# A parallel-head decoder step on 8 cores: the order of the opening phase rewritten (x tiles, first weights, units in pieces)

## The reference

```python
h = rmsnorm(x, norm_g)                      # 4096 channels
z = h @ w_in                                # 9728 columns: u, gate_a, glu_val, glu_gate, gate_b, q, gate_c
a = glu_val * sigmoid(glu_gate)             # then a causal depthwise conv of width 31, layer norm, silu, @ w_pw
k, v = rmsnorm(mem, mem_norm_g) @ w_mem_k, ... @ w_mem_v      # 256 memory tokens
y = rmsnorm(x + concat(pool(u)*silu(gate_a), conv(a)*silu(gate_b), attn(q,k,v)*silu(gate_c)) @ w_out)
```

## Time and profile before

| | us |
|---|---|
| median of 3 runs | 1980.24 (1979.48 to 1980.29) |
| the profiled execution, its time | 1981.93 |
| its slowest core (core 4), first to last instruction | 1980.4 |
| the other cores | 1962.9 to 1976.2 |
| TensorE busy on core 4 | 1853.8 |
| VectorE busy | 971.4 |
| ScalarE busy | 357.1 |
| DMA, mean rate | 131 GB/s |

### The profile page before, as it was taken

How to read it: one execution, slowest core, us unless ns; L and a number is a source line. 1 busy time by engine, 2 the same in 40 slices (tenths; PEclk the granted TensorE clock), 3 DMA queues, 4 the chain that set the end, 5 groups by cost and what they waited for, 6 DMA issues and landing times.

```text
span 1980.4 us, 29544 instructions; the slowest of 8 cores (1962.9 to 1980.4 us)
## 1 busy us (share of the span) xinstructions
PE 1853.8 (94%) x11388; PEld 941.7 (48%) x11592; DVE 971.4 (49%) x1367; ACT 357.1 (18%) x626; POOL 142.0 (7%) x270
## 2 busy tenths in 40 slices
PE   2768999899999999999999999999989999999997
PEld 1435555555444544544445555554444444444443
DVE  4548898848888888898580111121000110000355
ACT  4531011011011111011141232321000111111222
POOL 0000010110000000000001111100010000000000
PEclk9989999999999999999999999999999999999999
DMA  8854977695535444445446999745469577556897
GB/s 231 245 130 77 169 131 128 112 170 100 92 67 90 91 80 76 87 80 100 69 61 94 154 147 151 117 70 99 86 106 188 172 154 157 115 130 146 220 302 240
DMA packets 82091, 259.20 MB, mean 131 GB/s; under 512 B 12224, under 2 KB 18496, under 8 KB 76352
## 3 DMA queue, kind: packets, MB, share of 16 engines
q0 software_dynamic: 39328, 153.76, 48.6%
q1 hardware_dynamic: 42624, 103.53, 16.9%
HBM read 370.56 MB, written 40.45 MB: 208 GB/s over the span
## 4 chain that ended last, share of the span: by engine, by line
PE 88%; DMA 5%; DVE 3%; issue 2%; ACT 1%; DVEq 0%; SPq 0%; ACTq 0%; POOLq 0%
PE pz L364 77%; PE ps L364 10%; DMA slot<-w_in 2%; DVE HT L444 2%; DMA wo<-w_out 1%; ACT XN L425 1%; DMA XT<-x 1%; DMA slot<-w_mem_v 1%; PE ps L442 0%; DVE SQ L376 0%; DVE YB L497 0%; PE pz L442 0%; DVE CCA L386 0%; DVE HM L444 0%; ACT XN L420 0%
## 5 line engine op out<-in xcount | busy, mean ns | idle before, releaser
L364 PE MATMUL pz<-HT,slot 128*128 128x512 bf16 x4715 | 1132.6, 382 | 17.6 <-DMA slot<-w_in 3.9
L386 DVE SCALAR_TENSOR_TENSOR YB<-EA,CS,YB 128x512 f32<-128x512 f32 x720 | 480.5, 745 | 0.0
L364 PEld LDWEIGHTS pz<-HT,slot 128*128 128x128 bf16 x4864 | 331.3, 98 | 311.1 <-issue 21.2
L364 PE MATMUL ps<-HT,slot 128*128 128x64 bf16 (+1 forms) x2432 | 469.4, 199 | 5.1 <-ACT SGt L370 3.6
L364 PEld LDWEIGHTS ps<-HT,slot 128*128 128x128 bf16 x2432 | 233.6, 98 | 287.2 <-issue 13.5
L376 DVE TENSOR_TENSOR YT<-pz,XR 128x512 f32<-128x512 f32 (+1 forms) x54 | 37.3, 691 | 283.9 <-PE pz L364 236.6
L340 POOL DMA_DIRECT2D slot<-w_in x152 | 80.8, 533 | 1004.4 <-PE ps L364 757.6
L364 PE MATMUL pz<-wo,CCA 128*128 128x512 bf16 (+1 forms) x636 | 148.9, 382 | 1.7 <-ACT SGC L370 0.8
L364 PE MATMUL pz<-wo,CCB 128*128 128x512 bf16 (+1 forms) x635 | 147.7, 379 | 0.7
L370 ACT ACT_TABLE_LOAD x45 | 57.7, 1283 | 477.0 <-PE ps L364 245.1
L1000 ACT ACTIVATE JK<-YT 128x512 bf16<-128x512 f32 (+1 forms) x72 | 45.3, 630 | 436.7 <-DVE YT L376 436.7
(11 more groups left out here) (148 smaller groups left out, 1190.9 us busy)
## 6 DMA issues: line engine op xcount, KB each, us to landing
slot<-w_in POOLq DMA_DIRECT2D x152, 512.0 KB, 6.2
wo<-w_out POOLq DMA_DIRECT2D x32, 1024.0 KB, 18.4
XT<-x SPq DMA_DIRECT2D x8, 2048.0 KB, 13.8
XR<-x SPq DMA_DIRECT2D x64, 256.0 KB, 8.1
y<-YT SPq DMA_DIRECT2D x64, 256.0 KB, 8.2
YF<-y SPq DMA_DIRECT2D x24, 512.0 KB, 6.6
y<-YF SPq DMA_DIRECT2D x24, 512.0 KB, 9.3
slot<-w_mem_k POOLq DMA_DIRECT2D x16, 512.0 KB, 9.1
```

Source lines behind the costliest of these rows:

```text
L364: S.op("pe", lambda e: e.matmul(out, lhsT=lhsT, rhs=rhs, start=start, stop=stop), r=r, w=w, t=max(64, n) / 2400 + 0.0025)
L386: S.op("dve", lambda e: e.scalar_tensor_tensor(out=out, in0=a, scalar=s, in1=b, op0=op0, op1=op1), r=r, w=w, wa=wa, t=n / 960 + 0.13)
```

## The change

- x has three buffers XT (the third in the place of HM) and XN has three. Tile 8, the one of 96 tokens, comes first: in the new order n = 0 is tile 8, n = 1 to 8 are tiles 0 to 7, n = 9 and 10 are memory. norm_scale(n) issues the load of n + 3. The first load is issued ahead of the constants, the second when those have landed, the third when the first tile has.
- Two more slots lie where the pooling's buffers will be; they are used once. w_gate lets POOL issue slot loads two at a time: each time after the load of tile n = 2, 4, 6, 8 has landed.
- The first three units are gg0, vv0 and gg1 (u0 goes back to the planner's list). They run in pieces of 256 tokens, for tiles 6 and 7 of 128, and one of 96, each between transposes. The small parts of the evictions (halo and samples: gg_small, v_small) are written right behind the piece of 96, the main ones at the end.
- vv1 is run as the fourth unit, ahead of the planner's loop, which starts with pair 2. norm_scale and norm_transpose of the memory tokens are written behind it.
- ESA's first load is issued behind the first tile, the pooling weights' load behind the opening.

```diff
-        XT = [at("XT", R, [D], F32), at("XT", R + 16384, [D], F32)]
+        XT = [at("XT", R, [D], F32), at("XT", R + 16384, [D], F32), at("XT", R_YB + 5 * 4352, [D], F32)]
         XN, XNb = [], []
-        for i, oo in enumerate((R_YB + 4352, R_YB + 3 * 4352)):
+        for i, oo in enumerate((R_YB + 4352, R_YB + 3 * 4352, R_AT + 5440)):
             XN.append(raw("XN", oo, [D], BF16)[0])
             XNb.append([S.buf("XN%d_%d" % (i, h), [(oo + 4096 * h, oo + 4096 * h + 4096)]) for h in range(2)])
         IDF, IDFb = at("IDF", R_AT, [128], F32)
+        slots += [at("slot", R_AT + 13632 + 4096 * i, [2048], BF16) for i in range(2)]
 
...
-        free_slots = collections.deque(range(NSLOT))
+        wst = {"issue": 0, "get": 0, "limit": 0}
+        free_slots = collections.deque((0, 1, 2, 3, NSLOT, NSLOT + 1, 4, 5))
         load_slot = {}
 
         def w_fill():
             if recording:
                 return
-            while free_slots and wst["issue"] < len(loads):
+            while free_slots and wst["issue"] < min(len(loads), wst["limit"]):
                 k = wst["issue"]
                 wst["issue"] += 1
                 name, i = loads[k]
@@ -351,7 +352,8 @@
         def w_release(s):
             if recording:
                 return
-            free_slots.append(s)
+            if s < NSLOT:
+                free_slots.append(s)
             w_fill()
 
...
-        S.dma("sp", lambda e: e.dma_start(out=CS[:], in_=cs_d), w=[CSb])
-        S.dma("sp", lambda e: e.dma_start(out=IDF[:], in_=id_d), w=[IDFb])
-        S.op("dve", lambda e: e.tensor_copy(out=IDB[:], in_=IDF[:]), r=[IDFb], w=[IDb])
         S.op("dve", lambda e: e.memset(ONES[:], 1.0), w=[ONb])
-
-        def norm_load(i, src, rows):
-            b = i % 2
-            S.dma("sp", lambda e: e.dma_start(out=XT[b][0][0:rows, :], in_=src), w=[XT[b][1]])
-
-        def norm_scale(i, rows):
-            b = i % 2
-            xt, xtb, xn, xnb, nb = XT[b][0], XT[b][1], XN[b], XNb[b], NSTb[i]
+        ORD = (8, 0, 1, 2, 3, 4, 5, 6, 7, 9, 10)
+        TILES = [(x_d[128 * i:min(NT, 128 * i + 128), :], min(NT - 128 * i, 128)) for i in range(9)]
+        TILES += [(mem_d[0:128, :], 128), (mem_d[128:256, :], 128)]
+
+        def norm_load(n):
+            if n < 11:
+                src, rows = TILES[ORD[n]]
+                S.dma("sp", lambda e: e.dma_start(out=XT[n % 3][0][0:rows, :], in_=src), w=[XT[n % 3][1]])
+
...
+            xt, xtb, xn, xnb, nb = XT[n % 3][0], XT[n % 3][1], XN[(n + n // 9) % 3], XNb[(n + n // 9) % 3], NSTb[i]
...
+            norm_load(n + 3)
+
+        def norm_transpose(n, qs):
+            i, rows = ORD[n], TILES[ORD[n]][1]
+            xn, xnb = XN[(n + n // 9) % 3], XNb[(n + n // 9) % 3]
+            if i < 9:
+                gcol, dst, dstb, c0 = C_G, HT, HTb[i], 128 * i
+            else:
+                gcol, dst, dstb, c0 = C_MG, HM, HMb[i - 9], (i - 9) * 128
+            for q in qs:
+                if i < 9:
                     k = ps()
                     t16, tb = PS16[k], PSb[k]
                 else:
...
+        def gg_small(j, si):
+            b = j % 2
+            act(EA[b][:, 0:NH], PS[si][:, 0:NH], AF.Sigmoid, [PSb[si]], [EAb[b][0]], NH)
+            act(SGS[b][0][:], PS[si][:, NH:NH + NS], AF.Sigmoid, [PSb[si]], [SGS[b][1]], NS)
+
...
+        def v_small(j, si):
             b = j % 2
             ea = EAb[b][0]
             tt(EA[b][:, 0:NH], PS[si][:, 0:NH], EA[b][:, 0:NH], ALU.mult, [PSb[si], ea], [], NH, wa=[ea])
             tt(ESA[:, :, 30:34], PS[si][:, NH:NH + NS].rearrange("p (s r) -> p s r", s=16),
                SGS[b][0][:].rearrange("p (s r) -> p s r", s=16), ALU.mult, [PSb[si], SGS[b][1]], [ESAb], NS)
+
+        def v_main(j, zi):
+            b = j % 2
+            ea = EAb[b][0]
             tt(EA[b][:, NH:], PZ[zi][:, :], EA[b][:, NH:], ALU.mult, [PZb[zi], ea], [], NPR, wa=[ea])
...
+        def w_gate(n, upto):
+            S.deps("pool", [XT[n % 3][1]], [])
+            wst["limit"] = upto
+            w_fill()
+
+        norm_load(0)
+        S.dma("sp", lambda e: e.dma_start(out=CS[:], in_=cs_d), w=[CSb])
+        S.dma("sp", lambda e: e.dma_start(out=IDF[:], in_=id_d), w=[IDFb])
+        S.op("dve", lambda e: e.tensor_copy(out=IDB[:], in_=IDF[:]), r=[IDFb], w=[IDb])
+        S.deps("sp", [CSb], [])
+        norm_load(1)
+        S.deps("sp", [XT[0][1]], [])
+        norm_load(2)
+        FIRST = (U_GG, U_V, U_GG + 1)
+        fs = {}
+        rot["pz"] = 3
+
+        def piece(u, a, b):
+            if u not in fs:
+                fs[u] = [w_get("in", 2 * FIRST[u] + h) for h in range(2)]
+            if b == NT:
+                k = ps()
+                out, tb = PS[k][:, 0:NT - a], PSb[k]
             else:
-                norm_transpose(i, 128, C_MG, HM, HMb[i - 9], (i - 9) * 128, False)
-
-        stage_load()
-        stage_load()
+                k = None
+                out, tb = PZ[u][:, a:b], PZb[u]
+            for kc in range(32):
+                sl = fs[u][kc // 16]
+                view = slots[sl][0][:, :].rearrange("p (k n) -> p k n", k=16)
+                mm(out, view[:, kc % 16, :], HT[:, kc, a:b], kc == 0, kc == 31, [slots[sl][1]] + HTb[a // 128:(b + 127) // 128], [tb])
+            return k
+
+        def whole(n):
+            norm_scale(n)
+            norm_transpose(n, range(4))
+
+        whole(0)
+        esa_load(0)
+        whole(1)
+        w_gate(2, 2)
+        whole(2)
+        norm_scale(3)
+        norm_transpose(3, (0, 1))
+        w_gate(4, 4)
+        piece(0, 0, 256)
+        norm_transpose(3, (2, 3))
+        gg_small(0, piece(0, NPR, NT))
+        norm_scale(4)
+        norm_transpose(4, range(4))
+        piece(0, 256, 512)
+        w_gate(6, 6)
+        piece(1, 0, 256)
+        piece(1, 256, 512)
+        v_small(0, piece(1, NPR, NT))
+        whole(5)
+        whole(6)
+        piece(0, 512, 768)
+        piece(1, 512, 768)
+        w_gate(8, 8)
+        gg_small(1, piece(2, NPR, NT))
+        piece(2, 0, 256)
+        norm_scale(7)
+        norm_transpose(7, (0, 1))
+        piece(2, 256, 512)
+        norm_transpose(7, (2, 3))
+        piece(2, 512, 768)
+        norm_scale(8)
+        norm_transpose(8, (0, 1))
+        piece(0, 768, 896)
+        norm_transpose(8, (2, 3))
+        piece(1, 768, 896)
+        piece(2, 768, 896)
+        wst["limit"] = 1 << 30
+        for u in range(3):
+            piece(u, 896, 1024)
+            for sl in fs[u]:
+                w_release(sl)
+            if u == 0:
+                gg_main(0, 0)
+            elif u == 1:
+                v_main(0, 1)
+            else:
+                gg_main(1, 2)
         wp_load(0)
-        esa_load(0)
...
         eus_load(0)
-        first_seg(1, 1, NPR, 1, 1)
-        first_seg(2, 1, NPR, 2, 0)
-        first_seg(0, 2, NPR, 0, 0)
-        for s_ in fs[0:2]:
-            w_release(s_)
-        gg_evac(0, 0, 0)
-        first_seg(1, 2, NPR, 1, 1)
-        for s_ in fs[2:4]:
-            w_release(s_)
-        sync_est("dve")
-        v_evac(0, 1, 1)
-        first_seg(2, 2, NPR, 2, 0)
-        for s_ in fs[4:6]:
-            w_release(s_)
-        u_evac(0, 2, 0)
-        rot["ps"] = 1
-        tile_T(9)
-        tile_T(10)
-        S.t["dve"] = S.t["pe"]
+        S.t["dve"] = S.t["pe"] + 7.0
...
+        run_unit("vv", 1)
+        for n in (9, 10):
+            norm_scale(n)
+            norm_transpose(n, range(4))
+        al = collections.deque(a_units)
         kl = collections.deque(kv_units)
         ql = collections.deque(range(8))
-        j = 1
+        j = 2
```

More of the change, by code:

```diff
@@ L441, in norm_transpose @@
                     kc = q * 8 + k
-                    S.op("pe", lambda e, k=k, kc=kc, tv=tv: e.transpose(out=tv[:, k, 0:rows], in_=XN[b][0:rows, kc * 128:(kc + 1) * 128],
-                                                                        identity=IDB[0:rows, 0:rows]), r=[XNb[b][q // 2], IDb], w=[tb], t=0.06)
+                    S.op("pe", lambda e, k=k, kc=kc, tv=tv: e.transpose(out=tv[:, k, 0:rows], in_=xn[0:rows, kc * 128:(kc + 1) * 128],
+                                                                        identity=IDB[0:rows, 0:rows]), r=[xnb[q // 2], IDb], w=[tb], t=0.06)
                 S.op("dve", lambda e, q=q, tv=tv: e.tensor_tensor(
@@ L473, in esa_load, with gg_main @@
             S.dma("sp", lambda e: e.dma_start(out=ESA[:].rearrange("p s r -> p (s r)"), in_=scin_d[j]), w=[ESAb])
+        def gg_small(j, si):
+            b = j % 2
+            act(EA[b][:, 0:NH], PS[si][:, 0:NH], AF.Sigmoid, [PSb[si]], [EAb[b][0]], NH)
+            act(SGS[b][0][:], PS[si][:, NH:NH + NS], AF.Sigmoid, [PSb[si]], [SGS[b][1]], NS)
+        def gg_main(j, zi):
+            b = j % 2
+            act(EA[b][:, NH:NH + NPR], PZ[zi][:, :], AF.Sigmoid, [PZb[zi]], [], NPR, wa=[EAb[b][0]])
         def gg_evac(j, zi, si):
-            b = j % 2
             if j >= 2:
                 bg_need("conv%d" % (j - 2))
[L479 to L483, removed]
```

(29 more changed lines are left out.)

11 lines of the change are left out of this document (1 added, 10 removed).

## The result

| | before | after |
|---|---|---|
| median, us | 1980.26 | 2027.21 |
| ratio, with its 95% interval | | 1.0236 [1.0213, 1.0259] |
| the profiled execution, us | 1981.93 | 2028.07 |
| its slowest core (core 4), us | 1980.4 | 2026.5 |
| the eight cores, us | 1962.9 to 1980.4 | 2007.7 to 2026.5 |

The change costs 47 us. The forecast was 1998 (1983 to 2007): the sign was right, the size was not, and the time lies outside the range. Beside the ratio to the kernel before I give the mean of the eight cores' spans, averaged over executions: for most kernels it scatters by only 1 us, while the slowest core scatters by several.

The account below looks back on a forecast made before the run. TensorE, busy 1853.8 of 1980.4 us, was taken as the bound, with most winnable idle time in the opening. The opening's +17.4 and +0.4 behind it gave 1980.2 + 17.8 = 1998.0 us, range 1983 to 2007.

Parts of the forecast that it names:

- The term: Opening: four units and all tiles done at 191.1, where before four would be at 173.7; +17.4 us.
- the two causes: Opening: squares of later tiles queue behind small gate evictions on ScalarE; memory norm's reciprocal queues behind v_evac(1) on VectorE.
- First transpose at 9.8 + 7.9: Opening: first tile and constants there at 9.8, its first transpose 7.9 later, at 17.7.
- the next follow at 8.75: Opening: the next tiles are transposed at a cadence of 8.75, at 25.5, 34.3 and 43.0.
- The first two slots are issued at n = 2's landing, about 24, and have 20 us: Opening: the first unit's two weight-slot loads go out at about 24 and have 20 us.
- the tables: ScalarE, opening: each activation table switch costs the load's 1.28; four new switches on the chain are in the sum.
- switches cost double: Rival: a table switch between waiting instructions costs the load's length again, 5.1 more; time 2003, chance 0.05.
- The cold start: TensorE, opening: a piece begun at the lower clock takes 2.2 more; four such starts, 8.8 in the sum.
- Behind the opening ... I take +0.4 for all this: After the opening: new unit order, w_mem_v slot waits that stay and four gate-unit neighbours; +0.4, bounds −2 and +3.
- Memory norm hidden: Rival: the memory tokens' reciprocals get ahead of v_evac(1), 7.9 less; time 1990, chance 0.08.
- Cadence holds: Rival, opening: relief of the transfers decides and TensorE stays warm, 17.8 − 21.1 = −3.3; time 1976, chance 0.12.
- Absorbed: Rival: the opening's loss is given back where TensorE waits later, behind 160 us; time 1980, chance 0.07.

Follow-up runs that it names:

- e2: Changed kernel with norm_scale of n = 4, 5 and 7 written ahead of the pieces whose evictions they stood behind: ratio 1.0148, mean of cores −15.4.
- e3: Changed kernel with norm_scale(9) ahead of the fourth unit and norm_scale(10) between its matmuls and its eviction: ratio 1.0198, mean −5.8.
- e10: Changed kernel with the rest of conv1 written behind v0, ahead of v1: ratio 1.014, mean −19.0.
- e11: Changed kernel with w_out's first tiles laid over the weight slots in the order in which they come free: ratio 1.0202, mean −8.0.
- e6: Kernel before with its own opening, then the units in the changed kernel's order: ratio 1.007, mean of cores +13.3 against before.
- e7: Changed kernel with its own opening, then a list giving the units in the order of the kernel before: ratio 1.0158, mean −18.4.
- e8: Changed kernel with the edits of e2, e3, e9, e10 and e11 together: ratio 1.0018, mean 1967.1 against 1970.6 of before.
- e12: Changed kernel with the edits of e2, e3, e9 and e11, and e7's list of units: ratio 0.9996, mean 1965.8 against 1972.4 of before.
- e9: Changed kernel without SP's wait for the constants and with the first unit's slots requested a tile sooner: ratio 1.0218, mean −3.0.
- e4: Changed kernel without SP's wait for the constants ahead of the second x load: ratio 1.0219, mean −1.4.

## Why the prediction was right, and where it failed

**Right: the opening.** Start of the first transposes of tile n, in us:

| | T(0) | T(3) | T(4) | T(5) | T(7) | T(8) | k0 |
|---|---|---|---|---|---|---|---|
| predicted | 17.7 | 43.0 | 63.8 | 87.9 | 123.7 | 137.0 | 191.1 |
| after, median of cores | 18.7 | 44.7 | 66.5 | 90.0 | 124.5 | 136.9 | 191.0 |
| after, core 4 | 19.2 | 46.7 | 72.3 | 96.2 | 130.8 | 143.2 | 197.1 |

The term was +17.4; the cores' median is +15.6 and core 4 +23.3. On the median core no step is more than 2.7 off. That k0 comes out to 0.1 is in part luck: the steps up to T(4) were priced 2.7 too short and those from T(4) to T(8) 2.8 too long. The 1.8 between the terms is nearly all the base: I worked from core 4 of before, which began k0 at 189.1, 1.6 ahead of the median. e2 and e3 confirm the two causes. For core 4 two sizes were off. "First transpose at 9.8 + 7.9" and "the next follow at 8.75" left the gate on the constants out: the wait for x was 3.64. "The first two slots are issued at n = 2's landing, about 24, and have 20 us" gave them too little: issued at 30.33, the second one landed at 55.31, 25 later.

**Right: the tables.** The load at 68.16 takes 1.28 and the root runs at 69.45; ahead of the load the engine reads out the square's sum, from 67.88 for 0.20. The drain of about 1380 ns that the Trainium skill gives besides the load for every switch (ScalarE: Activation LUTs, What ACT_TABLE_LOAD costs) is on neither side of it, so the measurement decides against it; the rival "switches cost double" falls. The cold start measured 13.33 − 10.64 = 2.7 against 2.2.

**Wrong: "Behind the opening ... I take +0.4 for all this", bounds −2 and +3.** It was +30 by the median core. The order of units that I had worked out was the order that ran; the price I put on it wasn't. I read TensorE's waits of before in the earlier trace rows and asked how many of each kind there would be, as if a new order could bring only more of the old waits. The neighbouring gate units were priced well: SGt has 23.2 − 15.9 = 7.3 besides the stall, in four waits of 1.8, the four places that I had counted. What failed is that I priced the new order from TensorE's waits alone. Three things stood in none of the rows that I had read:
- *The stall, 19 us (e10).* To see it I had to follow three queues under the new order: the squares behind the copies on ScalarE, the copies behind stores for two staging buffers, and CCA behind 30 conv steps on VectorE. v0 and v1 had moved up next to the end of conv1; I noted the move and priced only slots and neighbours. A look at VectorE's waits for SQ in before would have shown the chain, at 402.22. e10 shows that it is queue order and not VectorE's amount of work: only the place of conv1's end was moved, and the wait went from 15.91 to 1.82. That ScalarE's and VectorE's queues are strictly first in, first out is what the Trainium skill says (PSUM — Partial Sum Buffer, Engine vs sequencer instructions); the 22.11 us of a still VectorE, with conv2's steps written behind, agree. I used that rule in the opening and not behind it.
- *w_out's first loads, 8 us (e11).* "Two more slots are used once" was in my front matter, and nothing in my sum asked who counts on the rotation 1400 us later.
- *The order's own waits.* w_mem_k, w_mem_v and gate neighbours: up to 13 in the kernel before (e6). In after they are smaller than e7's scatter of 3, since e7 (−18.4) gives no more than e10 (−19.0); e8 and e12 put them at some 4 us, 1802.9 against 1798.6 behind k0.

**The rivals.** *Memory norm hidden* was right as a price: 7.9 forecast, 6.7 at k0 in e3; but the changed kernel didn't do it. *Cadence holds* priced the order of the scalar queue at 21.1; e2 gave 16.8 at k0. *Absorbed* fell: e2's 16.8 came through as 15.4. No rival went beyond 2003, and the range's upper end had only the bounds of terms I had named; a mechanism that I hadn't named had no room in it.

## What to carry to other kernels

When a change reorders work far behind the place it rewrites, walk each engine's queue there as carefully as at the place itself: for each eviction, what is written ahead of it, and what that waits for. A buffer rotation is shared state: adding a slot that is used once shifts everyone who counts on which slot comes free when, here 1400 us later. And judge a change of a few us by all eight cores, not by the slowest: core 4 began k0 6 us behind the median, most of it a wait of 4.14 for one slot that only three of the eight cores had.

## What the runs showed of the hardware

- Constants queued behind a first x tile of 1.57 MB land with it: issued at 1.53 and 1.99 in after, the second x load, which waits for them, went out at 11.84, where the tile itself was there at 11.33.
- With the same program and issue times of 26.7 to 31.2, the second slot of the first unit made TensorE wait between 0 us (core 6) and 4.14 (core 4) in after. In e9, with the request one tile sooner, it was 0 on all eight.
- A core's opening hardly tells its end: core 7 began k0 at 189.9 and ended at 2020.9, core 3 at 196.4 and 2022.4. Much of the spread goes by pairs of neighbours, (0,1), (2,3), (4,5) and (6,7): in all four executions of after one core of each pair ends 5.9 to 13.3 us behind the other, and which one it is changes from execution to execution. In e4 the late four take 1833.2 behind k0 and the early four 1822.6, and TensorE's waits for loads there are 24.5 and 14.8 (w_out alone 13.0 and 7.0). Why one core of a pair gets its loads later no run took apart.
